# Pair 0 of every gated stage in eight direct half products

## The reference, cut to what matters

```python
def swiglu(h, w_gu, w_down):
    gt, up = jnp.split(h @ w_gu, 2, axis=-1)
    return (jax.nn.silu(gt) * up) @ w_down

def short_conv_mixer(h, w_in, w_conv, w_out):
    bg, cg, xv = jnp.split(h @ w_in, 3, axis=-1)
    return (bg * dwconv(cg * xv, w_conv, SC_PAD)) @ w_out

def reference(...):
    ...
        h = h + g1 * y
        h = h + g2 * swiglu(modulate(rmsnorm(h, norm2_g[l]), sh2, sc2), ffn_w_gu[l], ffn_w_down[l])
    ...
    return rmsnorm(h, final_g)
```

## Time and profile before

| | us |
|---|---|
| median of 3 runs | 2256.26 |
| lowest and highest | 2252.51 and 2260.28 |
| the profiled execution | 2250.08 |
| its span, first to last instruction | 2248.1 |
| its mean granted TensorE clock | 0.997 |
| TensorE busy in the span | 2179.8 |
| VectorE busy | 1675.7 |
| GpSimd busy | 1244.7 |
| ScalarE busy | 925.7 |

### The profile page before, as it was taken

One profiled execution on the slowest core, in us unless ns is written; L12 is line 12 of the kernel. 1 busy time (PEld: TensorE's weight loads), 2 busy tenths in 40 slices (PEclk: granted clock), 3 DMA queues, 4 the chain that ended last, 5 costly groups with the idle time before them and its releaser, 6 DMA issues.

```text
span 2248.1 us, 27764 instructions
## 1 busy us (share of the span) xinstructions
PE 2179.8 (97%) x9982; PEld 1767.9 (79%) x9982; DVE 1675.7 (75%) x1899; ACT 925.7 (41%) x1596; POOL 1244.7 (55%) x820
## 2 busy tenths in 40 slices
PE   8999999999999999999999899999899999999998
PEld 3788887878777888888888678888677888878886
DVE  5677865863788999997557997755978988877554
ACT  4555546862532223324445422234522333334443
POOL 3223313788566666667746355563366766657442
PEclk9999999999999999999999999999999999999999
DMA  9756558744346666668666233353245554567654
GB/s 340 226 151 179 165 169 199 165 143 136 127 136 229 216 216 222 222 219 291 196 190 196 61 104 103 116 175 107 71 161 196 190 187 166 187 229 235 196 188 150
DMA packets 364578, 402.01 MB, mean 179 GB/s; under 512 B 72127, under 2 KB 249499, under 8 KB 363547
## 3 DMA queue, kind: packets, MB, share of 16 engines
q1 hardware_dynamic: 326379, 376.65, 52.0%
q10 hardware_dynamic: 37488, 21.50, 3.4%
q0 software_dynamic: 576, 2.10, 0.2%
HBM read 294.52 MB, written 108.02 MB: 179 GB/s over the span
## 4 chain that ended last, share of the span: by engine, by line
PE 57%; POOL 14%; DVE 12%; DMA 9%; ACT 3%; issue 3%; SPq 1%; ACTq 0%; DVEq 0%; POOLq 0%
PE bank L1324 17%; PE bank L1326 17%; PE bank L1325 17%; POOL slot_lo L1230 6%; DMA pair_raw<-in_ffn_w_gu 5%; POOL slot L1230 4%; PE bank L1420 1%; POOL w_part L1243 1%; POOL w_part L1245 1%; DMA q_spill<-qk_raw 1%; DVE t_sum L2386 1%; POOL act_lo L1254 1%; PE bank L1561 1%; DVE t_sum L2393 1%; DVE act_lo L2426 1%
## 5 line engine op out<-in xcount | busy, mean ns | idle before, releaser
L1230 POOL TENSOR_TENSOR slot_lo<-pair_raw,slot_hi 128x512 fp32r<-128x512 f32 x112 | 169.1, 1510 | 290.9 <-ACT slot_hi L1849 290.9
L1230 POOL TENSOR_TENSOR slot<-pair_raw,slot 128x512 fp32r<-128x512 f32 x144 | 239.4, 1674 | 13.4 <-ACT slot L1849 13.4
L1849 ACT CAST slot_hi<-pair_raw 128x512 fp32r<-128x512 f32 x112 | 69.0, 616 | 363.6 <-DMA pair_raw<-in_ffn_w_gu 312.2
L1230 POOL TENSOR_TENSOR slot_lo<-t_sum,slot_hi 128x512 fp32r<-128x512 f32 x109 | 163.7, 1522 | 72.7 <-ACT slot_hi L1849 72.7
L1254 POOL TENSOR_TENSOR act_lo<-low_f,act_lo 128x512 fp32r<-128x512 f32 x96 | 135.7, 1425 | 112.5 <-ACT act_lo L1899 112.5
L1324 PE MATMUL bank<-a,slot_hi 128*128 128x512 f32 x436 | 173.6, 398 | 11.6 <-ACT zt L1869 7.2
L1324 PE MATMUL bank<-act_lo,slot_hi 128*128 128x512 f32 x436 | 171.1, 392 | 6.8 <-DVE act_lo L2426 5.9
L1326 PE MATMUL bank<-a,slot_hi 128*128 128x512 f32 x436 | 170.4, 391 | 0.0
L1325 PE MATMUL bank<-a,slot_lo 128*128 128x512 f32 x436 | 169.9, 390 | 0.0
L1326 PE MATMUL bank<-act_lo,slot_hi 128*128 128x512 f32 x436 | 169.8, 389 | 0.0
L1325 PE MATMUL bank<-act_lo,slot_lo 128*128 128x512 f32 x436 | 169.7, 389 | 0.0
(11 more groups left out here) (366 smaller groups left out, 6278.9 us busy)
## 6 DMA issues: line engine op xcount, KB each, us to landing
pair_raw<-in_ffn_w_gu SPq DMA_DIRECT2D x88, 512.0 KB, 4.3
z_parts<-zt SPq DMA_DIRECT2D x148, 256.0 KB, 4.5
mod_in_f<-in_mod_w SPq DMA_DIRECT2D x48, 512.0 KB, 6.2
w_part<-in_ffn_w_down SPq DMA_DIRECT2D x88, 256.0 KB, 4.6
w_sums<-w_part SPq DMA_DIRECT2D x88, 256.0 KB, 5.0
low_f<-z_parts SPq DMA_DIRECT2D x88, 256.0 KB, 3.0
mod_in_p<-in_mod_w SPq DMA_DIRECT2D x32, 512.0 KB, 4.5
low_f<-w_sums SPq DMA_DIRECT2D x48, 256.0 KB, 2.6
```

Of the source, the lines that this page charges most:

```text
L1230: nc.gpsimd.tensor_tensor(low, from_, high, ALU.subtract).then_inc(s_wlo, 1)
L1849: nc.scalar.copy(slot(st, n, p)[0], from_).then_inc(s_whi, 1)
```

## The change

Pair 0 of each stage is made of eight plain half products, without sums. The lower token half gives C11 (products 0 and 3 of pair 0, now added up in one bank, without a copy) and C12 (the second column block, two new entries `(4, 0)` and `(5, 0)` of `FIRST`, in bank 7). The upper token half, as plain tokens 7 (first four feature blocks) and 6 (last four), gives C21 and C22 in four direct products (`DIRECT`), from the same four weight operands. Pair 1 is the first that needs sums of tokens and of weights; its five summed products follow in the order 1, 2, 4, 5, 6. The list of VectorE's `joint` is reordered to low parts of 7 and 6 first. Loads of pair 0's two blocks and of pair 1's separate halves go; the list of first loads has ten entries, and ScalarE's casts of the last three wait for all ten. In F0 and F1 the gating of pair 0's lower token half is `gate_first`, inside `joint`; in S ScalarE copies C12 and C22 out of their banks (`quarter_copy`). Pair 1's products 2, 4, 5 and 6 go to banks that pair 0's quarters leave.

```diff
-        FIRST = ((0, 0), (0, 1), (3, 0), (0, 2), (3, 1), (0, 3), (3, 2), (3, 3))
+        FIRST = ((0, 0), (0, 1), (3, 0), (0, 2), (3, 1), (0, 3), (3, 2), (3, 3), (4, 0), (5, 0))
+        FIRST_SLOT = (0, 1, 2, 3, 4, 5, 6, 1, 3, 4)
+        FIRST_AFTER = (0, 0, 0, 0, 0, 0, 0, 2, 4, 5)
         REST = (1, 2, 4, 5, 6)
-        LEAD = ((1, 0), (2, 0), (1, 1), (4, 0), (6, 0), (5, 0))
-        MAKE = ((1, 0), (2, 0), (4, 0), (5, 0), (1, 1), (6, 0), (5, 1), (2, 1), (6, 1), (4, 1))
-        TOKENS = (1, 2, 4, 6, 5)
-        MOVED = {(4, 0): 3, (1, 1): 4, (5, 1): 0, (6, 1): 3}
+        DIRECT = ((0, 7), (4, 7), (3, 6), (5, 6))
+        MAKE = ((1, 1), (2, 1), (4, 1), (5, 1), (6, 1))
+        TOKENS = (7, 6, 1, 2, 4, 5)
+        MOVED = {(1, 1): 5, (2, 1): 6, (4, 1): 1, (5, 1): 0, (6, 1): 3}
...
-        BANKS = ({1: 2, 2: 1, 4: 6, 6: 0, 5: 1}, {1: 7, 2: 6, 4: 2, 5: 0, 6: 1}, {1: 7, 2: 1, 4: 6, 5: 2, 6: 1})
+        C12_BANK, C21_BANK, C22_BANK = 7, 2, 1
+        BANKS = (None, {1: 6, 2: 7, 4: 2, 5: 0, 6: 1}, {1: 7, 2: 1, 4: 6, 5: 2, 6: 1})
...
             7: [(act_hi[:, k, two], act_hi[:, 4 + k, two]) for k in range(4)],
...
-                load_pair(st, 0, 0)
-                load_pair(st, 0, 1)
+                load_pair(st, 1, 0)
+                load_pair(st, 1, 1)
...
-                load_first(st, 7)
+                for e in (7, 8, 9):
+                    load_first(st, e)
...
+            def direct_product(w_of, x_of, bank_, first, ready=None):
+                high, low = w_of
+                for k in range(4):
+                    if ready is not None:
+                        pe.wait_ge(*ready(k))
+                    w = (high[:, k * P:(k + 1) * P], low[:, k * P:(k + 1) * P])
+                    mm = product(bank[:, bank_, :], w, *ACTS[x_of][k], first and k == 0, not first and k == 3)
+                mm.then_inc(s_prod, 1)
...
                 if p == 0:
-                    part(1)
-                    part(2)
-                    part(1, 1)
-                    part(4)
-                    pe.wait_ge(*made(g, C11))
-                    part(6)
-                    pe.wait_ge(*made(g, U2))
-                    part(5)
+                    pe.wait_ge(s_nhi, 8 * (NORM[st] + 2))
+                    for i, (n, x) in enumerate(DIRECT):
+                        direct_product(slot(st, n, 0), x, C21_BANK if i % 2 == 0 else C22_BANK, i < 2, ready(x, 0))
                     return
                 if p == 1:
...
+                    gated = (0, PAIRS[F0], PAIRS[F0] + PAIRS[S] // 3)[st] + 1
+                    part(1)
+                    pe.wait_ge(*(quarter_copied(0) if st == S else (s_z0, gated)))
                     part(2)
-                    pe.wait_ge(*made(g - 1, C22))
+                    pe.wait_ge(*((s_z1, PAIR0[S] + 1) if st == S else (s_silu1, gated - (0 if st == F0 else FT // 2))))
                     part(4)
-                    pe.wait_ge(*made(g - 1, C21))
+                    pe.wait_ge(s_xfree, PAIR0[st] + 1)
                     part(5)
...
             def token_high(st, n, k):
...
+                if n in (4, 5):
+                    act.wait_ge(s_prod, direct_at(st, 1) + 1)
...
-                    act.wait_ge(s_first, 128 * st + (128 if e == 7 else 112))
+                    act.wait_ge(s_first, 16 * (len(FIRST) * st + (7 if FIRST.index((n, p)) < 7 else len(FIRST))))
...
+            def quarter_copy(which):
+
+                act.wait_ge(s_prod, product_at(S, 5, 0) + 1 if which == 0 else direct_at(S, 3) + 1)
+                nc.scalar.copy((c12, c22)[which], bank[:, (C12_BANK, C22_BANK)[which], :]).then_inc(s_p1, 1)
...
                 second_half(st, 3)
...
+                token_high(st, 7, 3)
+                operand_high(st, *FIRST[7])
+                for k in range(4):
+                    token_high(st, 6, k)
+                first_product_copied(st, 3)
+                operand_high(st, *FIRST[8])
+                operand_high(st, *FIRST[9])
+                token_high(st, 1, 0)
+                token_high(st, 1, 1)
+                operand_high(st, 1, 1)
...
+                for k in range(4):
+                    token_high(st, 4, k)
+                operand_high(st, 6, 1)
+                if st != S:
+                    silu_first(st, 0)
+                else:
+                    quarter_copy(0)
                 for k in range(4):
-                    token_high(st, 6, k)
-                for n in (2, 6, 4):
-                    operand_high(st, n, 1)
+                    token_high(st, 5, k)
...
                 for k in range(4):
                     if k < 3:
                         scale(n + 1, *order[2 * k + 2])
+                        scale(n + 1, *order[2 * k + 3])
+                    token_low(st, 7, k)
+                for k in range(4):
                     token_sum(st, 1, k)
-                    if k < 3:
-                        scale(n + 1, *order[2 * k + 3])
+                    token_low(st, 6, k)
+                for k in range(4):
                     token_sum(st, 2, k)
+                    token_low(st, 1, k)
                 for k in range(4):
-                    token_low(st, 1, k)
-                weight_sum(st, 1, 1)
+                    token_sum(st, 4, k)
                 for k in range(4):
                     token_sum(st, 5, k)
                     token_low(st, 2, k)
-                token_sum(st, 4, 0)
                 for k in range(4):
-                    if k < 3:
-                        token_sum(st, 4, k + 1)
                     token_low(st, 4, k)
-                pair_first(st, 0, zt[:, 0, one])
...
+                if st != S:
+                    gate_first(st)
                 for k in range(4):
                     token_low(st, 5, k)
 
+            def gate_first(st):
+                dve.wait_ge(s_xfree, PAIR0[st] + 1)
+                dve.wait_ge(s_prod, product_at(st, 5, 0) + 1)
+                V.tensor_tensor(zt[:, 0, one], zt[:, 0, one], bank[:, C12_BANK, :], ALU.mult).then_inc(s_z0, 1)
...
+                if p == 0 and kind == "gate":
+                    dve.wait_ge(s_silu1, gated + 1 - (0 if st == F0 else FT // 2))
+                    dve.wait_ge(s_prod, direct_at(st, 3) + 1)
+                    V.tensor_tensor(z_two, z_two, bank[:, C22_BANK, :], ALU.mult).then_inc(s_z1, 1)
+                    return
+                if p == 0:
+                    dve.wait_ge(*quarter_copied(0))
+                    V.tensor_tensor(c12, x, c12, ALU.mult).then_inc(s_xfree, 1)
+                    dve.wait_ge(*quarter_copied(1))
+                    V.tensor_tensor(c22, bank[:, C21_BANK, :], c22, ALU.mult).then_inc(s_z1, 1)
+                    last_taps(tile)
+                    return
                 before_pair(st, p)
...
```

More of the change, by code:

```diff
@@ L454, in slot_at @@
                 return MOVED[n, p]
-            return FIRST.index((n, p)) % 7 if p < EARLY and n in (0, 3) else n
+            return FIRST_SLOT[FIRST.index((n, p))] if (n, p) in FIRST else n
         BESIDE = 6
@@ L492, in made @@
         def made(g, what):
-            order = (C11, U2, U3, U4, C22, C21, C12) if g in PAIR0 else (C11, U2, U4, U3, C22, C12, C21)
-            return s_made, 7 * g + order.index(what) + 1
+            before = sum(g > first for first in PAIR0)
+            return s_made, 7 * (g - before) + (C11, U2, U4, U3, C22, C12, C21).index(what) + 1
         c12, c22 = t_pad[:, 1:1 + HALF], t_pad[:, 1 + HALF:1 + SEQ]
@@ L506, in backbone @@
             6: [(a22[:, k // 2, k % 2 * HALF:(k % 2 + 1) * HALF], a22[:, 2 + k // 2, k % 2 * HALF:(k % 2 + 1) * HALF]) for k in range(4)],
+            7: [(act_hi[:, k, two], act_hi[:, 4 + k, two]) for k in range(4)],
         }
@@ L1222, in operand_low @@
                 at_, (high, low) = operand_at(st, n, p), slot(st, n, p)
-                if p < EARLY and n in (0, 3):
+                if (n, p) in FIRST:
                     from_ = slot_full(slot_at(n, p))
@@ L1303, in _ @@
                     first_lows(st)
-                operand_low(st, *FIRST[7])
-                for n, p in MAKE:
+                for n, p in (*FIRST[7:], *MAKE):
                     operand_low(st, n, p)
@@ L1664, in first_products @@
                 c11(1, {2: lambda: norm_spread(n)})
-                for e in range(2, 8):
+                for e in range(2, len(FIRST)):
                     c11(e)
@@ L1831, in operand_high @@
                 g, s = PAIR0[st] + p, slot_at(n, p)
-                early = p < EARLY and n in (0, 3)
-                if early:
-                    e = FIRST.index((n, p))
-                    act.wait_ge(s_first, 128 * st + (128 if e == 7 else 112))
+                if (n, p) in FIRST:
+                    act.wait_ge(s_first, 16 * (len(FIRST) * st + (7 if FIRST.index((n, p)) < 7 else len(FIRST))))
                     from_ = slot_full(s)
@@ L1868, in silu_first @@
                 to = zt[:, p % 2, one]
-                nc.scalar.activation(to, bank[:, x_bank(p), :] if p else to, ACT.Silu).then_inc(s_xfree, 1)
```

(23 more changed lines are left out.)

220 lines of the change are left out of this document (100 added, 120 removed).

## The result

| | before | after |
|---|---|---|
| median, us (20 runs each) | 2254.76 | 2259.64 |
| lowest and highest | 2251.02, 2260.28 | 2255.16, 2263.10 |
| span of the profiled execution | 2248.1 | 2254.8 |
| its mean granted clock | 0.997 | 0.992 |

The ratio is 1.0021 with a 95% interval of 1.0014 to 1.0028: 4.9 us slower, within the 0.3% of the prediction's middle case. The forecast of 2257 us in a range of 2246 to 2267 holds. As a change it said +1.1 us; the three runs of the kernel before that it was put on have a median 1.5 us above that of the twenty. The way there was another than the one forecast, in two of its steps.

The account below looks back on a forecast made before the run. VectorE's queue was taken to bound each stage's start; F0 +0.8, S -0.5 and F1 +0.8 us, +1.1 us on 2250.1 us, gave 2251.2, or 2257 us on the runs' scale (median 2256.3), range 2246 to 2267.

Parts of the forecast that it names:

- the prediction's middle case: Whole kernel: time the same, within about 0.3% or 6.8 us of no change; chance 0.65.
- VectorE's queue sets the start of a stage: First scaled feature to last low part: VectorE busy 40.8 of 41.3 us, TensorE waiting wherever that queue has not reached.
- The wait for the tenth load: ScalarE's cast of FIRST[7]: load lands about 600.1, TensorE's last early product 1.1 us late, VectorE waits until 601.35.
- The queue from there to the gate: VectorE from 601.35 to gate_first: 31 operations, 18.6 us, gate 0.7, 7.5 GpSimd meetings 8.3 us; gate ends at 629.0.
- The wait is moved, not removed: Pair 1's product 2 waits 3.6 us for gate_first; 0.6 us won in F0, 1.3 us in S.
- From pair 2 on ... nothing: Later waits move along with pair 1's end, no added cost; pair 2's loads about 623, some 4 us earlier.
- The clock: TensorE's clock halves after the new idle times: 1.4 us charged a stage, 0.8 us in S.
- The eighth half product fills a wait: Pair 0: 12 added matmuls, 2.74 us a stage, fill a wait if the queue TensorE waits for is no shorter.
- The sum: Stages F0 +0.8, S -0.5, F1 +0.8 us: +1.1 us in all.
- the waits vanish: Rival: VectorE reaches the gate by 625.4; F0 and F1 win 4.4 us each, S 6.1; 2241 us, chance 0.18.
- The slow tenth load: Rival: each microsecond beyond 3.0 delays all three stages; at 6.0 us +9 us, 2266 us; chance 0.17.
- that rival: Rival that the clock stays, with no fall behind the new waits: -2.5 us, 2254 us; chance 0.20.

Follow-up runs that it names:

- e1: Changed kernel with ScalarE's cast of FIRST[7], which waits for the tenth load, behind the tokens 6 casts and product 0's copy; 0.9983 of the kernel before.
- e9: Changed kernel plus five VectorE memsets, with gate and first SiLU (S: c12, c22 and their copies) earlier; ScalarE's tenth-load wait still first; 1.0006 of the kernel before.
- e10: e9 without the five memsets: gate early, ScalarE's cast behind the tenth load still ahead of the casts of tokens 6; 0.9977 of the kernel before.
- e11: The kernel of e8 measured again, beside e10 on one chip; 0.9936 of the kernel before.
- e2: Changed kernel with five one-column memsets in VectorE's joint, behind token sums 4 and each low part of tokens 2; 1.0003 of the kernel before.
- e3: Changed kernel with twelve filler matmuls on TensorE in the wait for pair 1's C22; 1.0017 of the kernel before.
- e4: Changed kernel with three of four blocks of pair 0's last direct product left out, 27 matmuls in three stages; 1.0013 of the kernel before.
- e7: The changed kernel itself measured again, beside e5; 1.0013 of the kernel before.
- e8: e1 with VectorE's gate and ScalarE's first SiLU (S: products c12, c22 and their copies) moved earlier, no memsets; 0.9923 of the kernel before.
- e5: Changed kernel with the edits of e1 and e2 together; 0.9960 of the kernel before.

## Why the prediction came out

The total was right, the mechanism half, so the hit is in part luck. Point by point:

- **VectorE's queue sets the start of a stage**: right, and more so than the text used. By e1, e9 and e10 it holds back the pairs behind too, through their sums and loads.
- **The wait for the tenth load**: right in place and size. FIRST[7] was cast at 604.06, 600.2 on the old scale (forecast 600.1); VectorE waited 3.46 us (3.5); TensorE's last early product lost 1.1 us (1.1). As a cause it was priced only by way of the gate; e10 and e11 give it 3.1 us a stage by way of VectorE's queue and pair 2's sums.
- **The queue from there to the gate**: mis-sized. 24.2 us to the gate's start against 26.9 forecast. The 1.1 us a meeting holds (e2), the count does not: five meetings, not seven and a half, because GpSimd's last three low parts were held off altogether. This step supposed that who comes second waits for one instruction; in a run without a break GpSimd waited for fifteen. By the prediction's own test, no wait above 1 us in pair 1, the queue was mis-added: TensorE's wait there is 0.4 us in F0 and F1 and 1.0 in S.
- **The wait is moved, not removed**: right in kind, wrong in place. Not 3.6 us at the gate but 2.1 to 3.3 us a pair later, at C22.
- **"From pair 2 on ... nothing"**: the step that failed. It put pair 2's loads 4 us earlier (about 623); they went out at 634.05, 630.2 on the old scale, where the kernel before has them at 624.8 and 627.7, and the first sums of pairs 2 and 3 came 0.7 and 2.0 us later than before. The text looked for the next late thing on TensorE alone; it was on VectorE, beside it.
- **The clock**: it fell behind a wait in each stage, to 0.51, as charged, but behind C22, and of the 0.9 to 2.6 us that it took at the spot only 0.4 to 0.6 us a stage was left far into the pairs, within the scatter of profiles (e3).
- **The eighth half product fills a wait**: right (e4).
- **The sum**: +0.8, -0.5 and +0.8 us forecast for the stages, +3.0, -0.6 and +0.5 measured (e7: +2.4, -0.6, +1.3). Two errors of some 3 us, the gate too dear and pair 2 too cheap, nearly cancel; that the total came out rests on this. The medians' 4.9 us has 2 us more than the stages; whether they lie ahead of F0 one profile of before can't tell.
- **Rivals**: "the waits vanish" (2241) needed a queue 3.6 us shorter or no wait for the tenth load. In e8, without that wait and with the gate early, it is so: 2237.5 us where before had 2253.9 on that chip. e1 alone, the condition as the text put it, gave less (0.9983): in F0 pair 2's first sum comes 2.1 us earlier than before, in e8 4.4 us. The slow tenth load did not come (cast at the forecast time); the clock fell, so that rival is out too.

The Trainium skill (SBUF — State Buffer, section "SBUF: two separate sides") says that the shared pair goes to whichever of the two starts first, for a whole instruction, and the other fully blocks. The trace agrees for a single meeting: GpSimd's operation from 614.37 in the change took 1.31 us, and VectorE's from 614.43 1.80 us in place of 0.60. That VectorE's next instruction takes the pair again ahead of a GpSimd instruction that already waits, up to 10.1 us on end and 12.5 us in S, the section does not say, and the prediction did not read into it.

## What to carry to other kernels

When a queue is the bound, a wait taken off TensorE is only worth what the queue itself gets shorter: follow the queue past the point where TensorE is let go, to the next loads that hang on it. An instruction that waits for a transfer belongs behind the work that others wait for: moving one cast behind five instructions was worth 9 us here (e10 against e11). Between VectorE and GpSimd, look who must win: a long run of two-input instructions keeps GpSimd out, and one instruction of another kind in the right place lets it in.

## What the runs showed of the hardware

- GpSimd's low part of weights, at most 1.9 us in the kernel before, lasted 10.1 to 12.5 us while VectorE ran instructions with two SBUF inputs back to back. In four cases it ended 1.2 us after the first VectorE instruction of another kind: one that reads PSUM, or a memset of one column.
- Once GpSimd is in, the two take turns: in the change its next two operations took 1.7 us each, beside VectorE's four in 5.17 us (2.49 us undisturbed).
- A wait of 1.9 us at the gate in e5 was followed by a granted clock of 1.00 in F0 and of 0.66 over the next 3 us in F1 (below): the idle time alone doesn't tell a fall here.

Busy time behind those two gates in e5 (columns as above):

```profile
629.20:632.20 3.00, 3.00 (x15) 2.45 (x14) 2.96 (x6) 0.00 (x0) 0.34 (x1) 1.00 0.23 87
1620.60:1623.60 3.00, 3.00 (x11) 2.34 (x10) 2.96 (x6) 0.00 (x0) 0.37 (x1) 0.66 0.23 87
```
